# Product-key experts: one product of 512 columns for two of 256, its halves added on VectorE

## The reference, cut to what matters

```python
def step(args):
    x_c, e_c, g_c = args
    a = jnp.einsum('cd,ced->ce', x_c, u[e_c])
    w = jax.nn.gelu(a.astype(jnp.float32), approximate=False).astype(x_c.dtype) * g_c
    return jnp.einsum('ce,ced->cd', w, v[e_c])
```

```
a[e, t]   = sum over d of u_key[d, e] * x[d, t]        first product of a key
w[e, t]   = gelu(a[e, t]) * gate[key, e, t]
y[t, :]  += sum over e of w[e, t] * v_key[e, :]        second product of a key
```

## Time and profile before

| | us |
|---|---|
| median of 3 runs (2997.16 to 3000.37) | 2999.04 |
| the profiled execution, as timed | 3001.94 |
| its span, first to last instruction | 3000.2 |
| first matmul of key 0's first product | at 596.60 |
| last matmul of key 127's second product | at 1320.09 |

### The profile page before, as it was taken

One profiled execution on the slowest core, in us unless ns is written; L12 is line 12 of the kernel. 1 busy time (PEld: TensorE's weight loads), 2 busy tenths in 40 slices (PEclk: granted clock), 3 DMA queues, 4 the chain that ended last, 5 costly groups with the idle time before them and its releaser, 6 DMA issues. The chain is left out here.

```text
span 3000.2 us, 41196 instructions
## 1 busy us (share of the span) xinstructions
PE 2525.0 (84%) x15704; PEld 1765.9 (59%) x15704; DVE 1141.1 (38%) x2376; ACT 657.8 (22%) x1231; POOL 126.6 (4%) x180
## 2 busy tenths in 40 slices
PE   5667796699999999969968699898865867999885
PEld 2245664589999999956835455444434545544442
DVE  2251396766666666643431411111135223111112
ACT  0030005844444444423201100000013011000000
POOL 0130000000000000000200000000002000000000
PEclk9888898999999999989989799999978887999998
DMA  5303331055554555564134199999930532999995
GB/s 181 139 1 113 125 128 68 21 182 182 186 191 182 187 190 182 188 229 148 59 119 182 39 427 427 428 426 427 409 120 35 207 106 122 427 426 427 427 427 241
DMA packets 128755, 654.57 MB, mean 218 GB/s; under 512 B 15472, under 2 KB 17904, under 8 KB 93680
## 3 DMA queue, kind: packets, MB, share of 16 engines
q1 hardware_dynamic: 115424, 625.64, 52.5%
q10 hardware_dynamic: 13200, 27.10, 2.6%
HBM read 643.92 MB, written 8.78 MB: 218 GB/s over the span
## 5 line engine op out<-in xcount | busy, mean ns | idle before, releaser
L436 PE MATMUL banks<-weight_ring,window_rows_T 128*64 128x256 f32 x2496 | 286.9, 384 | 45.1 <-DMA weight_ring<-in_moe_w_up 28.6
L436 PE MATMUL banks<-peer_input_high,u_high 128*128 128x256 f32 x1024 | 290.4, 284 | 14.8 <-DVE u_low L1173 14.8
L436 PE MATMUL banks<-peer_input_high,u_low 128*128 128x256 f32 x1024 | 290.7, 284 | 0.0
L436 PE MATMUL banks<-peer_input_low,u_high 128*128 128x256 f32 x1024 | 290.6, 284 | 0.0
L2466 DVE COPY expert_hidden_T<-banks 128x256 f32<-128x256 f32 x64 | 27.2, 424 | 678.3 <-PE banks L2328 678.3
L436 PEld LDWEIGHTS banks<-weight_ring,window_rows_T 128*64 128x64 f32 x2496 | 188.7, 138 | 157.2 <-issue 42.6
L436 PEld LDWEIGHTS banks<-peer_input_high,u_high 128*128 128x128 f32 x1024 | 197.0, 192 | 20.5 <-DVE u_low L1173 15.6
L436 PE MATMUL banks<-v_high,gated_high 128*128 128x512 f32 x512 | 200.9, 392 | 0.0
L436 PE MATMUL banks<-v_low,gated_high 128*128 128x512 f32 x512 | 200.8, 392 | 0.0
L436 PEld LDWEIGHTS banks<-peer_input_low,u_high 128*128 128x128 f32 x1024 | 197.0, 192 | 4.7
L436 PE MATMUL banks<-v_high,gated_low 128*128 128x512 f32 x512 | 199.2, 389 | 0.0
(11 more groups left out here) (454 smaller groups left out, 3489.6 us busy)
## 6 DMA issues: line engine op xcount, KB each, us to landing
weight_ring<-in_moe_w_down SPq DMA_DIRECT2D x42, 2048.0 KB, 35.4
weight_ring<-in_moe_w_gate SPq DMA_DIRECT2D x40, 2048.0 KB, 35.4
weight_ring<-in_moe_w_up SPq DMA_DIRECT2D x38, 2048.0 KB, 34.4
u_of_key<-in_peer_u_T SPq DMA_DIRECT2D x128, 512.0 KB, 4.3
v_of_key<-in_peer_v_rows SPq DMA_DIRECT2D x128, 512.0 KB, 3.5
more_weight_slots<-in_moe_w_up SPq DMA_DIRECT2D x26, 2048.0 KB, 33.5
more_weight_slots<-in_moe_w_gate SPq DMA_DIRECT2D x24, 2048.0 KB, 35.3
more_weight_slots<-in_moe_w_down SPq DMA_DIRECT2D x22, 2048.0 KB, 35.4
```

Source lines behind the costliest of these rows:

```text
L436: return k.nc.tensor.matmul(out, lhsT, rhs, start=start, stop=stop)
```

## The change

The high and the low activations go side by side into one tile, `peer_input_high_low`, of 512 columns for each chunk. `pre` multiplies `u_high` by all 512 columns in one matmul, which fills the whole bank, and `u_low` by the 256 columns of the high part, into the bank's first half: 16 matmuls for 24. The two halves of the bank now have to be added, since high by high plus low by high is in the first, high by low in the second. A new step `add` on VectorE copies the second half into `key_sums` (raising `halves_copied`), waits for its own copy, and adds the first half (raising `key_sums_ready`). The gelu reads `key_sums` in SBUF and not the bank, and waits for `key_sums_ready`, as does the first product that takes the bank again. `add` of key n+2 stands at the head of `dve_step` of n.

```diff
-        hT_high, hT_low = (k.sb(f"peer_input_{n}", [P, DC, S], F32R, ctx=c) for n in ("high", "low"))
+        hT_both = k.sb("peer_input_high_low", [P, DC, 2, S], F32R, ctx=c)
+        hT_high, hT_low = (hT_both[:, :, n, :] for n in range(2))
...
             pe.wait_ge(k.u_low_ready.sem, k.u_low_ready.at(n + 1))
             if not start:
-                pe.wait_ge(k.act_ready.sem, k.act_ready.at(n - 3))
-            out = k.ps[:, 4 + b, 0:S]
+                pe.wait_ge(k.key_sums_ready.sem, k.key_sums_ready.at(n - 3))
+            out = k.ps[:, 4 + b, :]
             for ch in range(DC):
                 high, low = (as_u(t, b % 2)[:, ch, :] for t in parts[0])
-                h_high, h_low = hT_high[:, ch, :], hT_low[:, ch, :]
-                mm(k, out, high, h_high, ch == 0, False)
-                mm(k, out, high, h_low, False, False)
-                last = mm(k, out, low, h_high, False, ch == DC - 1)
+                nc.tensor.matmul(out, high, hT_both[:, ch, :, :].rearrange("p a t -> p (a t)"), start=ch == 0, stop=False,
+                                 skip_group_check=True)
+                last = nc.tensor.matmul(out[:, 0:S], low, hT_both[:, ch, 0, :], start=False, stop=ch == DC - 1,
+                                        skip_group_check=True)
             last.then_inc(k.products.up(), 1)
...
-            act.wait_ge(k.products.sem, k.products.at(n + 1))
+            act.wait_ge(k.key_sums_ready.sem, k.key_sums_ready.at(n + 1))
             if not start:
                 act.wait_ge(k.weights_gated.sem, k.weights_gated.at(n - 1))
-            nc.scalar.activation(gelu[:, b % 2, :], k.ps[:, 4 + b, 0:S], ACT.Gelu).then_inc(k.act_ready.up(), 1)
+            nc.scalar.activation(gelu[:, b % 2, :], total[:, b % 2, :], ACT.Gelu).then_inc(k.act_ready.up(), 1)
...
+        def add(dve, n, b, start):
+
+            dve.wait_ge(k.products.sem, k.products.at(n + 1))
+            if not start:
+                dve.wait_ge(k.act_ready.sem, k.act_ready.at(n - 1))
+            nc.vector.tensor_copy(total[:, b % 2, :], k.ps[:, 4 + b, S:2 * S]).then_inc(k.halves_copied.up(), 1)
+            dve.wait_ge(k.halves_copied.sem, k.halves_copied.at(n + 1))
+            nc.vector.tensor_tensor(total[:, b % 2, :], k.ps[:, 4 + b, 0:S], total[:, b % 2, :],
+                                    ALU.add).then_inc(k.key_sums_ready.up(), 1)
...
         def dve_step(dve, i, b):
 
             n = TURN * i + b
+            if i is not LAST or b + 2 < TURN:
+                add(dve, n + 2, (b + 2) % TURN, i is FIRST and b + 2 < 2)
             if i is not LAST or b + 1 < TURN:
                 gate(dve, n + 1, (b + 1) % TURN, i is FIRST and b + 1 < 2)
                 low(dve, 1, n + 1, (b + 1) % TURN)
...
         @block.vector
         def _(dve):
             low(dve, 0, 0, 0)
             low(dve, 0, 1, 1)
+            add(dve, 0, 0, True)
             gate(dve, 0, 0, True)
             low(dve, 1, 0, 0)
             low(dve, 0, 2, 2)
+            add(dve, 1, 1, True)
```

More of the change, by code:

```diff
@@ L241, in __init__ @@
         self.small_loaded = signal("small_loaded")
+        self.halves_copied = signal("halves_copied")
+        self.key_sums_ready = signal("key_sums_ready")
         self.scores_ready = signal("scores_ready")
@@ L1094, in _ @@
             def _(act):
-                nc.scalar.activation(hT_high[:, :, :], hT[:, :, :], ACT.Copy).then_inc(k.act_ready.up(), 1)
+                nc.scalar.activation(hT_high, hT[:, :, :], ACT.Copy).then_inc(k.act_ready.up(), 1)
             @block.vector
@@ L1099, in _, with peer_steps @@
                 dve.wait_ge(k.act_ready.sem, k.act_ready.at(1))
-                nc.vector.tensor_tensor(hT_low[:, :, :], hT[:, :, :], hT_high[:, :, :],
+                nc.vector.tensor_tensor(hT_low, hT[:, :, :], hT_high,
                                         ALU.subtract).then_inc(k.dve_step.up(), 1)
         c2.close()
-        gelu, w = (k.sb(n, [P, 2, S], ctx=c) for n in ("gelu_out", "gated"))
+        gelu, w, total = (k.sb(n, [P, 2, S], ctx=c) for n in ("gelu_out", "gated", "key_sums"))
         w_high, w_low = (k.sb(n, [P, 2, S], F32R, ctx=c) for n in ("gated_high", "gated_low"))
-        peer_steps(k, gates, raw, parts, hT_high, hT_low, gelu, w, w_high, w_low)
-def peer_steps(k, gates, raw, parts, hT_high, hT_low, gelu, w, w_high, w_low):
+        peer_steps(k, gates, raw, parts, hT_both, total, gelu, w, w_high, w_low)
+def peer_steps(k, gates, raw, parts, hT_both, total, gelu, w, w_high, w_low):
     nc = k.nc
@@ L1261, in _ @@
                     dve_step(dve, i, b)
-            for sig in (k.weights_gated, k.u_low_ready, k.v_low_ready):
+            for sig in (k.weights_gated, k.u_low_ready, k.v_low_ready, k.halves_copied, k.key_sums_ready):
                 sig.repeated(turns - 2, TURN)
```

## The result

The changed kernel takes 3235.6 us (3233.4 to 3236.8), the kernel before 2999.1: a ratio of 1.0788, with a 95% interval of 1.0770 to 1.0807. It is 236.5 us slower. The forecast was 3250, with 3222 to 3305.

A forecast was written before the change was run, and what follows sets the result against it. TensorE bounds the old kernel; the change makes first products and VectorE's steps wait on each other, 1.99 us more a key. 249 + 0.9 + 0.8 = 251 us over the median 2999.0 gives 3250, range 3222 to 3305.

The forecast's parts named there:

- The bound and the place: VectorE's work, about 4.35 us a key, fits under TensorE's 5.54 by totals, but not with `add` at its step's head.
- The ring: First product, add, gate, `v_low`, `u_low`, next first product wait on each other: 7.62 us a key against 5.63.
- first product, to its last matmul's start: On TensorE, from a first product's start to the start of its last matmul: 2.77 us a key.
- last matmul and the signal to VectorE: The first product's last matmul, 0.28 us, and TensorE's signal to VectorE, 0.21: 0.49 us a key.
- copy and addition: `add`'s two instructions on VectorE: copy 0.46 us and addition 0.34, together 0.80 a key.
- gate: VectorE's three steps before `v_low`, queued behind `add`: 0.34 + 0.46 + 0.34 = 1.14 us a key.
- signal to TensorE: From the end of `u_low` on VectorE to the next first product's first matmul on TensorE: 0.05 us.
- The ends: Extra time at the stage's start, 0.9 us, and at its end, 0.8 us.
- TensorE's own gain: Eight merged matmul pairs a key save 0.088 us, 11 us over 128 keys, if TensorE stays the bound.
- The load: Rival: SyncE's loads of u and v set the pace; every second `u_low` 0.4 us late, 25 us, 3275; 8%.
- The faster rival: `u_low` of n+3 comes in time, TensorE stays the bound and keeps its 11 us: 2988 us; 2%.
- The clock rival: TensorE's clock falls to 1.2 GHz in gaps of 2 us; 2.6 us per such key, one in four, 3334; 8%.

The follow-up runs named there:

- e1_add_last: The changed kernel with `add` of key n+2 moved from the head to the end of VectorE's step, behind `u_low` of n+3: 3016.7 us, ratio 1.0067.
- e7_half_copy: The changed kernel with a second copy of only 128 columns, into an unread tile, ahead of `add`'s own copy: 3338.0 us, ratio 1.1128.
- e4_extra_copy: The changed kernel with a second copy of the bank's second half (256 columns), into an unread tile, ahead of `add`'s own: 3370.4 us, ratio 1.1244.

## Why the prediction was right

**The bound and the place.** The prediction's main step was that VectorE's list, and not its load, decides. The wait alone (3158.8) and the addition in another place (2998.9 with the same instructions) show it from both sides.

**The ring, term by term**, from the key shown above (907.82 to 915.31) and as means over some 124 keys of the stage:

| step | forecast | that key | mean |
|---|---|---|---|
| first product, to its last matmul's start | 2.77 | 2.75 | 2.80 |
| last matmul and the signal to VectorE | 0.49 | 0.41 | 0.34 |
| copy and addition | 0.80 | 0.80 | 0.80 |
| gate | 1.14 | 1.13 | 1.13 |
| `v_low`, up to `u_low` | 1.14 | 1.13 | 1.13 |
| `u_low` | 1.23 | 1.22 | 1.22 |
| signal to TensorE | 0.05 | 0.05 | 0.07 |
| sum | 7.62 | 7.49 | 7.49 |

Over 125 keys (606.91 to 1544.39) the ring is 7.50. The 0.12 us that it was forecast too long are 15 us, and this is nearly the whole of the miss (3250 for 3235.6). It comes from the signal, which was 0.15 shorter than forecast on average, while the first product was 0.03 longer. I had taken 0.21 between a second product's end and the gate; here the copy began 0.04 after the last matmul's end in one key (903.08 + 0.28 to 903.40) and 0.13 in the other, 0.06 on average. The signal to TensorE was 0.05 in one key and 0.14 in the other (906.46 + 1.22 to 907.82). The first matmul after the wait took 0.33 to the next, as forecast.

**The ends.** Forecast 0.9 and 0.8. Key 2's first product began 0.89 later counted from the stage's first matmul (606.91 - 596.86 against 605.76 - 596.60). The last first product's start to the last matmul's took 11.69 against 10.96, 0.7 more.

**TensorE's own gain.** This step failed. 0.088 us a key were forecast, 0.028 measured without the addition. The sum of steps took the step of 512 columns as fixed, and it is not: the merged first product saved 0.062 and not 0.088, and the second product beside it took 0.034 more. The Trainium skill's fixed cost of about 2.5 ns for each matmul (TensorE: Matmul & The Clock Gate, "Wait — 56ns, not 53.3ns?") gave 0.020. That is nearer to the 0.028 of a whole key, but by chance in part: the first product alone saved 0.062 over eight merged pairs, 7.8 ns each. In the ring the failed term is the 0.03 us by which the first product was longer than forecast, some 4 us in all, and the signal more than made up for it.

**The rivals.** The load did not decide in the changed kernel (`u_low` waited for `u_high` once, 1.4 us), but a ring through the loads was real in a neighbour, e1_add_last. The faster rival named the right point, the place of the addition, but promised too much: with the place mended the kernel is level with the one before. The clock rival did not come in, and my reason against it was weak. I had argued from a busy share of 74% at a clock of 1.00; e7_half_copy has 78% and a clock of 0.91. Part of its 78% is the slower matmuls themselves: the changed kernel's 5.8 us of TensorE in a key would be 76% of the 7.71 us of its keys at full clock. That is still above the 74%. The price was off too: 2.6 us for a key with a fall were forecast and 1.4 measured, since it was mostly the first product that ran at the lower clock (25 of 126 second products had such steps in e4_extra_copy), and TensorE kept a gap. The Trainium skill (same page, "A second HAM failure mode: psum-queue depth-cycling") tells of a kernel in which short idle spells between groups of matmuls make the clock swing. The changed kernel did not behave so (1.00 with gaps of 1.6 to 1.7 us in every key behind the first four), and the two with a copy more did. That the clock held was in part luck: the forecast had a ring of 7.62 us and a gap of about 2 us, between the 7.50 at which it held and the 7.71 at which it fell, and nothing in the prediction told on which side. The rival deserved more than 8%.

## What to carry to other kernels

Before an instruction is put at the head of an engine's list, ask what it waits for, what is queued behind it, and whether any of that is wanted by the engine it waits for. If so a ring closes, and its length, not any engine's total work, is the pace. Here the same two instructions cost 237 us at the head of the step, 18 us at its end, and nothing between its fourth and fifth instruction. And a gap that repeats on TensorE has a second price: add up the ring first, then look at the granted clock, since 0.2 us more in each key cost 27 us by itself here and 76 through the clock.

## What the runs showed of the hardware

- TensorE's clock held at 1.00 in the changed kernel from 616 us to the stage's end, with a gap of 1.59 to 1.74 us in each key (1.46 in the first). In key 2 of the same kernel, behind a gap of 2.12, it fell for some 3 us (from 608.05, a mean of 0.83 over 606 to 616). With 0.2 us more in the ring it fell in 54 of 124 first products, behind gaps of 1.79 to 1.94 us and one of 2.63 (mean 0.91 in the stage). With 0.34 more it fell in 62 of 124, behind 1.92 to 2.06 (0.90). In both kernels gaps as long (up to 1.92 and 2.03) were also followed by a first product at full clock. It stayed at 0.99 when matmuls that nobody uses filled most of the gap. There the fall had cost 88 us (3370.4 against 3282.7); the same filling in the changed kernel, where nothing fell, cost nothing that could be measured (3238.6 against 3235.6).
- One matmul of 512 columns for two of 256 on the same weights, in a stream where each has its own weight load, made the first product 0.062 us shorter, 7.8 ns for each pair merged. The second product, which had not been edited, took 0.034 more, so that 3.5 ns for each pair are left. The reason for the second product's part is open.
- From the end of a matmul to the VectorE instruction that waits for it: 0.03 to 0.13 us over 124 keys of the changed kernel, 0.06 on average, and 0.21 in the key of the earlier trace rows.
